# A mixture-of-experts layer on one core: the router cut by row tiles, token rows fetched through a slot table, results stored by token and choice

## The reference, cut to what matters

```
x = x + mixed @ w_out
x2 = rmsnorm(x, g_ffn)                       # 336 x 1024
logits = x2 @ w_router + b_router            # 32 experts
top_v, top_i = lax.top_k(logits, 4); gates = softmax(top_v)
# every token goes to 4 experts: 1344 (token, choice) pairs
for each expert e, over its tokens:
    gu  = xb @ w_gu[e] + b_gu[e]             # 1024 -> 2048
    hid = (clip(up, -7, 7) + 1) * min(gate, 7) * sigmoid(1.702 * gate)
    y   = hid @ w_dn[e] + b_dn[e]            # 1024 -> 1024
x = x + sum over the 4 choices of gate * y;  output rmsnorm(x, g_final)
```

## Time and profile before

| | us |
|---|---|
| median of 3 runs (lowest, highest) | 1863.03 (1858.05, 1866.95) |
| the profiled execution, its own time | 1850.85 |
| its span | 1849.3 |
| PE busy in the span | 1625.6 (88%) |
| granted TensorE clock, mean over the span | 0.946 of full |
| bytes moved by DMA | 511.30 MB, mean 276 GB/s |

### The profile page before, as it was taken

How to read it: one execution, slowest core, us unless ns; L and a number is a source line. 1 busy time by engine, 2 the same in 40 slices (tenths; PEclk the granted TensorE clock), 3 DMA queues, 4 the chain that set the end, 5 groups by cost and what they waited for, 6 DMA issues and landing times.

```text
span 1849.3 us, 20445 instructions
## 1 busy us (share of the span) xinstructions
PE 1625.6 (88%) x7088; PEld 741.2 (40%) x7089; DVE 369.4 (20%) x899; ACT 372.1 (20%) x722; POOL 116.3 (6%) x220
## 2 busy tenths in 40 slices
PE   6999999999999967988789998787999987999980
PEld 4565665566666442322223333222333322333330
DVE  3343442232321143101001111000101110110114
ACT  2443342345330020101011111011111110111111
POOL 0100000000000002000000000000000000000003
PEclk9989999899999967989999999999999998999995
DMA  6586333121235327999999899999998999599984
GB/s 221 156 220 159 111 83 114 47 75 40 92 131 209 151 114 264 409 405 410 403 412 351 336 393 408 407 410 407 363 401 326 403 412 405 217 346 402 356 337 153
DMA packets 115685, 511.30 MB, mean 276 GB/s; under 512 B 11617, under 2 KB 15566, under 8 KB 82878
## 3 DMA queue, kind: packets, MB, share of 16 engines
q1 hardware_dynamic: 98772, 454.90, 62.8%
q0 software_dynamic: 16640, 55.81, 10.6%
q10 hardware_dynamic: 234, 0.08, 0.0%
HBM read 471.21 MB, written 39.55 MB: 276 GB/s over the span
## 4 chain that ended last, share of the span: by engine, by line
PE 67%; DMA 21%; DVE 5%; issue 3%; SPq 2%; ACT 1%; POOL 0%; DVEq 0%; POOLq 0%; ACTq 0%
PE bank L535 31%; DMA ring<-in_w_gate_up 20%; PE bank L870 17%; PE bank L893 11%; PE bank L539 3%; PE bank L861 2%; PE bank L876 1%; SPq L514 1%; ACT r_kv L955 1%; DVE r_c L1221 1%; DVE r_kv L1215 1%; DVE r_qk L1215 1%; SPq L518 1%; DVE r_qk L1221 1%; DVE ring L1215 0%
## 5 line engine op out<-in xcount | busy, mean ns | idle before, releaser
L870 PE MATMUL bank<-ring,r_kv 128*64 128x512 f32 x2184 | 511.1, 613 | 65.9 <-DMA ring<-in_w_gate_up 65.8
L893 PE MATMUL bank<-ring,r_kv 128*64 128x512 f32 x1248 | 297.9, 610 | 29.7 <-ACT r_kv L955 29.7
L870 PEld LDWEIGHTS bank<-ring,r_kv 128*64 128x64 f32 x2184 | 159.7, 140 | 391.0 <-issue 298.7
L535 PE MATMUL bank<-r_xt,ring 128*128 128x336 f32 (+2 forms) x896 | 267.0, 453 | 2.0 <-DVE r_xt L1218 1.6
L1215 DVE TENSOR_SCALAR r_kv<-bank 128x512 f32<-128x512 f32 (+1 forms) x80 | 54.6, 683 | 976.9 <-PE bank L876 963.7
L535 PEld LDWEIGHTS bank<-r_xt,ring 128*128 128x128 f32 (+2 forms) x896 | 164.8, 187 | 90.7 <-issue 17.1
L893 PEld LDWEIGHTS bank<-ring,r_kv 128*64 128x64 f32 x1248 | 91.9, 142 | 206.9 <-issue 206.0
L955 ACT ACTIVATE r_xt<-bank 128x512 f32<-128x512 f32 x39 | 23.3, 597 | 507.6 <-PE bank L893 507.6
L535 PE MATMUL bank<-ring 128*128 128x336 f32 (+4 forms) x336 | 97.9, 434 | 4.1 <-DVE ring L1374 3.9
L1174 ACT ACTIVATE r_o<-r_kv 128x512 f32<-128x512 f32 x39 | 24.6, 632 | 332.7 <-DVE r_kv L1215 332.7
L1647 POOL DMA_DIRECT2D y_rows<-r_xt x78 | 41.8, 536 | 638.3 <-ACT r_xt L955 635.6
(11 more groups left out here) (213 smaller groups left out, 967.6 us busy)
## 6 DMA issues: line engine op xcount, KB each, us to landing
ring<-in_w_gate_up SPq DMA_DIRECT2D x256, 1024.0 KB, 19.4
ring<-in_w_down SPq DMA_DIRECT2D x128, 1024.0 KB, 19.2
ring<-in_w_in SPq DMA_DIRECT2D x12, 2048.0 KB, 9.1
r_v<-x_rows POOLq DMA_DIRECT2D x41, 256.0 KB, 6.7
y_rows<-r_xt POOLq DMA_DIRECT2D x78, 128.0 KB, 5.4
x_rows<-r_c POOLq DMA_DIRECT2D x7, 1024.0 KB, 6.9
x_rows<-r_c POOLq DMA_DIRECT2D x9, 768.0 KB, 8.8
y_rows<-r_c POOLq DMA_DIRECT2D x1, 5376.0 KB, 29.9
```

What stands on the lines that cost most here:

```text
L535: ins = pe.matmul(out, l, r, start=(n == 0), stop=(n == len(pairs) - 1), **kw)
L870: ins = pe.matmul(half(gate_bank if q < 2 else up_bank, q % 2), xg[:, k, :], w[:, 512 * q:512 * q + 512], start=False, stop=False, skip_gr ...
L893: ins = pe.matmul(half(out_bank, t), hidT[:, j, BLK * h:BLK * h + BLK], w[:, h, 512 * t:512 * t + 512], start=(j == 0 and h == 0), stop=(j ...
```

## The change

- **Order of the router.** PE takes `out` of tiles 0 and 1, then the router of tile 0, then `out` of tile 2, then the router of tiles 1 and 2. DVE and ACT follow in the same manner, tile by tile. The one-hot rows of a tile are one instruction of 128 elements and one reduction.
- **Tables.** One bank `pos` holds positions and counts, and two small matmuls (`pend`, `be`) give the expert of each block. New is a table of slots: DVE builds `inslot` (12 x 128) and `spread` (12 x 110), and PE multiplies them (`tab`, 12 matmuls); the result says for each slot of each block which row of `x2` it takes, and which row of `y_rows` its result goes to. Empty slots get an index past the end (slot 0 of a block always has a valid one).
- **Rows in.** POOL writes `x2` to DRAM unscattered (3 DMAs), and each block's rows come by one indirect load with a bounds check that skips indices past the end. In the loop POOL first copies the block's column of indices to `now`.
- **Rows out.** Each block's 128 half rows (2 KB each) go by one indirect store to `y_rows`, which is now ordered by token and choice; empty slots are skipped.
- **No zeros.** The filling of `x_rows` and `y_rows` is gone.
- **End.** SP loads the results in 6 plain DMAs (two choices of one tile each, 1 MB for a tile of 128), DVE waits for each pair of choices, and SP stores the outputs.

The diff, cut to its core:

```diff
-    j += [("out", t, s) for t in range(3) for s in range(2)]
-    j += [("x2T", t, s) for t in range(3) for s in range(2)]
-    j += [("lg", t) for t in range(3)] + [("pos", t) for t in range(3)] + [("cnt",)]
-    j += [("gT", t) for t in range(3)] + [("bd", t, s) for t in range(3) for s in range(2)]
+    for t in range(2):
+        j += [("out", t, s) for s in range(2)]
+    j += [("x2T", 0, 0), ("x2T", 0, 1), ("lg", 0), ("out", 2, 0), ("out", 2, 1)]
+    for t in (1, 2):
+        j += [("x2T", t, 0), ("x2T", t, 1), ("lg", t)]
+    j += [("pos",), ("pend",), ("be",), ("tab",), ("gT",)] + [("bd", t, s) for t in range(3) for s in range(2)]
...
+            nb = sp.value_load(nbi[0:1, 0:1].bitcast(I32), min_val=NE, max_val=MAXB)
+            sp.wait_ge(m_store, 16 * nb)
+            for t, (c0, m) in enumerate(ROWS):
+                for q in range(2):
+                    sp.dma_start(ring[0:m, t * SLOT + 2048 * q:t * SLOT + 2048 * q + 2048],
+                                 y_rows_dram[8 * c0:8 * c0 + 8 * m, :].rearrange("(t h) d -> t (h d)", h=8)[
+                                     :, 2048 * q:2048 * q + 2048]).then_inc(fin_y[2 * t + q], 16)
...
-            pe.wait_ge(chosen_set, 3)
+            out_rows(0)
+            out_rows(1)
+            pe.wait_ge(ld_late, 64)
+            router(0)
+            out_rows(2)
+            router(1)
+            router(2)
+            b = begin("pos")
             for t, (c0, m) in enumerate(ROWS):
-                b = begin("pos", t)
-                pairs = [(cst("ones")[0:ROWS[s][1], 0:m], chosen[0:ROWS[s][1], s, :]) for s in range(t)]
-                pairs += [(cst("below")[0:m, 0:m], chosen[0:m, t, :])]
-                end(group(b[0:m, 0:NE], pairs), "pos", t)
-            b = begin("cnt")
-            end(group(b[:, 0:NE], [(cst("ones")[0:n, :], chosen[0:n, t, :]) for t, (_, n) in enumerate(ROWS)]), "cnt")
+                pe.wait_ge(chosen_set, t + 1)
+                group(b[:, NE * t:NE * t + NE],
+                      [(cst("ones")[0:ROWS[s][1], :], chosen[0:ROWS[s][1], s, :]) for s in range(t)]
+                      + [(cst("below")[0:m, :], chosen[0:m, t, :])])
+            group(b[:, 3 * NE:4 * NE], [(cst("ones")[0:n, :], chosen[0:n, t, :]) for t, (_, n) in enumerate(ROWS)])
+            end(group(b[0:NE, 4 * NE:4 * NE + 1],
+                      [(chosen[0:n, t, :], cst("ones")[0:n, 0:1]) for t, (_, n) in enumerate(ROWS)]), "pos")
+            pe.wait_ge(nblkT_set, 1)
+            b = begin("pend")
+            end(group(b[0:NE, 0:1], [(cst("below")[0:NE, 0:NE], nblkT[:, :])]), "pend")
+            pe.wait_ge(cmpT_set, 1)
+            b = begin("be")
+            end(group(b[:, 0:NB1], [(cst("ones")[0:NE, :], cmpT[:, :])]), "be")
+            pe.wait_ge(tab_d, 1)
+            b = begin("tab")
+            end(group(b[:, 0:2 * NB1], [(inslot[0:m, 4 * t + k, :], spread[0:m, 4 * t + k, :])
+                                        for t, (_, m) in enumerate(ROWS) for k in range(4)]), "tab")
...
+            norm_x1(0)
+            norm_x1(1)
+            x2_turned(0)
+            norm_x1(2)
+            x2_turned(1)
+            x2_turned(2)
...
-                for k in range(4):
-                    step(ts(onehot[0:m, t, k, :], cst("expert")[0:m, :], topif[0:m, t, k:k + 1], ALU.is_equal))
-                c = chosen[0:m, t, :]
-                step(tt(c, onehot[0:m, t, 0, :], onehot[0:m, t, 1, :], ALU.add))
-                step(tt(c, c, onehot[0:m, t, 2, :], ALU.add))
-                signal(tt(c, c, onehot[0:m, t, 3, :], ALU.add), chosen_set, t + 1)
+                step(tt(onehot[0:m, t, :, :], cst("expert")[0:m, :].unsqueeze(1).broadcast_to([m, 4, NE]),
+                        topif[0:m, t, 0:4].unsqueeze(2).broadcast_to([m, 4, NE]), ALU.is_equal))
+                signal(dve.tensor_reduce(chosen[0:m, t, :], onehot[0:m, t, :, :].rearrange("p k e -> p e k"),
+                                         AX.X, ALU.add), chosen_set, t + 1)
...
+            dve.wait_ge(ld_late, 64)
+            for t in range(2):
+                out_rows(t)
+                norm_x1(t)
+            choose(0)
+            out_rows(2)
+            norm_x1(2)
+            choose(1)
+            choose(2)
+            filled(dve, "pos")
+            pos = bank(("pos",))
+            thr = cst("thr")
+            step(tt(cmp6[0:NE, 0, :], pos[0:NE, 4 * NE:4 * NE + 1].broadcast_to([NE, 6]), thr[0:NE, :], ALU.is_gt))
+            signal(dve.tensor_reduce(nblkT, cmp6[0:NE, 0, :], AX.X, ALU.add), nblkT_set, 1)
+            step(tt(cmp6, pos[:, 3 * NE:4 * NE].unsqueeze(2).broadcast_to([128, NE, 6]),
+                    thr.unsqueeze(1).broadcast_to([128, NE, 6]), ALU.is_gt))
+            step(dve.tensor_reduce(nblk, cmp6, AX.X, ALU.add))
             step(dve.tensor_tensor_scan(pend, cst("ones")[:, 0:NE], nblk, 0.0, ALU.mult, ALU.add))
             step(tt(start, pend, nblk, ALU.subtract))
+            take(stt(posm, start.unsqueeze(1).broadcast_to([128, 3, NE]), float(BLK),
+                     pos[:, 0:3 * NE].rearrange("p (t e) -> p t e", t=3), ALU.mult, ALU.add), "pos")
+            filled(dve, "pend")
+            take(tt(pendT, bank(("pend",))[0:NE, 0:1], nblkT, ALU.add), "pend")
+            signal(ts(cmpT, cst("block", NE), pendT, ALU.is_ge), cmpT_set, 1)
+            step(tt(prod, onehot, posm.unsqueeze(2).broadcast_to([128, 3, 4, NE]), ALU.mult))
+            step(dve.tensor_reduce(dest, prod, AX.X, ALU.add))
...
+            step(tt(valc, cst("tok"), slotc, ALU.subtract))
+            step(tt(spread[:, :, 0:NB1], inblk, valc.unsqueeze(2).broadcast_to([128, 12, NB1]), ALU.mult))
+            step(tt(val4, cst("tok4"), slotc, ALU.subtract))
+            step(tt(spread[:, :, NB1:2 * NB1], inblk, val4.unsqueeze(2).broadcast_to([128, 12, NB1]), ALU.mult))
+            signal(tt(inslot, cst("slot").unsqueeze(1).broadcast_to([128, 12, 128]),
+                      slotc.unsqueeze(2).broadcast_to([128, 12, 128]), ALU.is_equal), tab_d, 1)
...
+            filled(dve, "tab")
+            tab = bank(("tab",))
+            step(ts(idxf[:, 0, :], tab[:, 0:NB1], cst("pad")[:, 0:1], ALU.add, cst("pad")[:, 2:3], ALU.min))
+            signal(dve.tensor_copy(idx[:, 0, :].bitcast(U32), idxf[:, 0, :]), idx_set, 1)
+            take(ts(idxf[:, 1, :], tab[:, NB1:2 * NB1], 2.0, ALU.mult, cst("pad")[:, 1:2], ALU.add), "tab")
+            signal(dve.tensor_copy(idx[:, 1, :].bitcast(U32), idxf[:, 1, :]), idx_set, 2)
...
-            pool.wait_ge(rows_zeroed, 16 * 17)
-            for t, (_, m) in enumerate(ROWS):
-                pool.wait_ge(desti_set, t + 1)
-                for k in range(4):
-                    pool.indirect_dma_start(
-                        x_rows_dram[:, :], bass.IndirectOffsetOnAxis(ap=desti[0:m, t, k:k + 1].bitcast(U32), axis=0),
-                        x2[0:m, t, :], None).then_inc(x_sent, 16)
-            pool.wait_ge(x_sent, 16 * 12)
-            pool.dma_start(xrow, x_rows_dram[0:BLK, :]).then_inc(m_xrow, 16)
+            for t, (c0, m) in enumerate(ROWS):
+                pool.wait_ge(x2_ready, t + 1)
+                pool.dma_start(x_rows_dram[c0:c0 + m, :], x2[0:m, t, :]).then_inc(x_sent, 16)
+            def rows_in(column):
+                pool.indirect_dma_start(xrow, None, x_rows_dram[:, :],
+                                        bass.IndirectOffsetOnAxis(ap=column[0:BLK, :].bitcast(U32), axis=0),
+                                        bounds_check=NT - 1, oob_is_err=False).then_inc(m_xrow, 16)
+            pool.wait_ge(x_sent, 48)
+            pool.wait_ge(idx_set, 2)
+            rows_in(idx[:, 0, 0:1])
             pool.wait_ge(moe_tab, 1)
             nb = pool.value_load(nbi[0:1, 0:1].bitcast(I32), min_val=NE, max_val=MAXB)
             pool.sem_inc(yrow_free, 1)
             pool.wait_ge(m_gath, 1)
-            pool.dma_start(xrow, x_rows_dram[BLK:2 * BLK, :]).then_inc(m_xrow, 16)
+            rows_in(idx[:, 0, 1:2])
             with pool.Fori(0, nb) as b:
-                src = x_rows_dram[bass.ds(pool.snap(b * BLK + 2 * BLK), BLK), :]
-                dst = y_rows_dram[bass.ds(pool.snap(b * BLK), BLK), :]
                 pool.wait_ge(m_gath, b + 2)
-                pool.wait_ge(moe_tab, 1)
-                pool.dma_start(xrow, src).then_inc(m_xrow, 16)
+                pool.wait_ge(m_xrow, 16 * b + 32)
+                pool.sem_inc(pool_goes, 1)
+                pool.tensor_copy(now[:, 0:1].bitcast(U32), idx[:, 0, bass.ds(pool.snap(b + 2), 1)].bitcast(U32)
+                                 ).then_inc(idx_now, 1)
+                pool.wait_ge(idx_now, 2 * b + 1)
+                pool.sem_inc(pool_goes, 1)
+                rows_in(now[:, 0:1])
                 pool.wait_ge(m_yrow, b + 1)
-                pool.wait_ge(moe_tab, 1)
-                for h in range(2):
-                    pool.dma_start(dst[:, 512 * h:512 * h + 512], yrow[BLK * h:BLK * h + BLK, :]).then_inc(m_store, 16)
-                pool.wait_ge(m_store, 32 * b + 32)
```

(20 more changed lines are left out.)

180 lines of the change are left out of this document (90 added, 90 removed).

## The result

| | before | after |
|---|---|---|
| median (lowest to highest), us | 1860.54 (1858.03 to 1866.95), 4 runs | 1831.01 (1828.35 to 1831.61), 4 runs |
| the profiled execution, its own time | 1850.85 | 1828.35 |
| its span | 1849.3 | 1826.5 |

The ratio is 0.9843, interval 0.9821 to 0.9865; the medians differ by 29.5 us. The forecast was 1849 us, a gain of 14, and a range of 1834 to 1860.

The account below looks back on a forecast made before the run. The prediction had PE bound 67% of the chain and DMA 21%, mostly in the expert loop. Router 1.5, loop bytes 6.5 and end 6 sum to a gain of 14, from 1863 to 1849 us; range 1834 to 1860.

Parts of the forecast that it names:

- The early part: Before `out`: the removed zero fills were hidden behind ACT and PE, so dropping them gains 0.
- The router up to the choices: From `out` to the last choices: new tile order and cheaper one-hots, with an assumed clock drop, gain 0.5 us.
- From the choices to the loop: Counts, slot tables, gates and `bd` before the loop: it starts at 712.4 instead of 713.9, gain 1 us here.
- The loop's bytes: Expert loop: skipped empty slots (46%) save DMA time in the DMA-bound stretches, gain 6.5 us.
- I take the middle: Loop bytes: 6.5 us chosen between 0, if neighbouring slots share an engine, and the full saving.
- The upper end: Loop bytes: saving if skipped rows thin all 16 engines, 12.8 us by bytes or 15.6 by DMA engine time.
- In the others only PE counts: Expert loop: fewer bytes save time only in DMA-bound stretches (641 us); elsewhere PE alone sets the time.
- The loop's hand-overs: Expert loop: index copies and indirect DMAs come about 1 us later, but PE waits for neither; cost 0.
- The end: Behind the loop: SP's plain loads start VectorE 5.4 us earlier and its last store saves 0.5; gain 6 us.
- Both pay: Rival: skipped bytes give 13 to 15.6, router clock 3 to 8, plus the end; gain 20 to 30; chance 0.27.
- Only the end pays: Rival: skipped slots and router order save nothing, gain 6 us, total 1857; chance 0.21.
- the late store: Rival: a block's indirect store lands late, PE waits before `down` in PE-bound blocks; 18 us slower, 1881; chance 0.07.

Follow-up runs that it names:

- e7: The changed kernel with the zero fills of before written again, to DRAM nothing reads, and their waits: 1828.87 us, ratio 0.9825.
- e8: The changed kernel with the router in the order of before (all three tiles stage by stage): 1825.95 us, ratio 0.9815.
- e2: The changed kernel with full loads: empty slots load row 335 of x2, stores still skip: 1850.25 us, ratio 0.9951.
- e3: The changed kernel with full stores: empty slots are written to spare rows behind y_rows, loads still skip: 1837.84 us, ratio 0.9885.
- e9: The changed kernel with full loads landing on partitions 0-31 and 96-127, turned by a selection product; stores skip: 1850.52 us, ratio 0.9936.
- e13: The changed kernel with full loads as 128 half rows on all 128 partitions, 4 transposes of 128 x 128; stores skip: 1825.54 us, ratio 0.9821.
- e17: The kernel before, its direct loads landing as 128 half rows on 128 partitions, turned by 4 transposes; nothing skipped: 1842.21 us, ratio 0.9904.
- e1: The changed kernel with no empty slot skipped, in loads or stores: 1853.55 us, ratio 0.9969.
- e14: The changed kernel with loads as half rows on 128 partitions; loads and stores both skip: 1818.63 us, ratio 0.9793.
- e11: The changed kernel with a third router order (tile 2's `out` split around tile 1's turning; ACT copies before normalizing tile 2): 1819.47 us, ratio 0.9770.
- e6: The kernel before, unaltered, profiled a second time: 1859.22 us, ratio 0.9985.
- e18: The changed kernel with the end's DMAs (6 loads, 4 stores) issued by POOL instead of SP: 1841.61 us, ratio 0.9891.

## Why the prediction was wrong

- **The early part: 0.** Right. e7 shows it.
- **The router up to the choices: 0.5.** From the start of `out` to the end of the counts it was 67.3 us before and is 66.5, so 0.7: right in size, but by luck. With the order of before (e8) this part takes 65.0, so the cheaper choices and counts gave 2.3 and the new order, whose gain was to come from here, took 1.5 back. The clock fell in the idle stretch and came back in `out` of tile 2, as assumed (15.5 us for 16.3). The stretch between the two `out` took 7.5 instead of 5.6, as the logits of tile 0 already ran at half clock.
- **From the choices to the loop: 1.** Nothing: 28.8 us in both. `tab` started 9.8 us behind the counts (forecast 9.2) and took 5.3 to 5.5 (4.6 to 5). In e8 the same tables took 26.2 us, since PE was at full clock for a few microseconds there; "`tab` wakes the clock" was named as a bound and happens with e8's order only.
- **The loop's bytes: 6.5.** This is the step that failed: 20.8. Three things were wrong in it.
  - "I take the middle" rested on an end of 0, should neighbouring slots share an engine; e2 and e3 show that both skips pay.
  - The upper end, 12.8 by bytes or 15.6 by the queue's time, priced a loaded row at its own packet. It costs more, since the weights beside it slow from 314 to 513 ns while rows land on partitions 0 to 63. e2 shows the size (19 us for the loads, against 7 for the stores), e9, e13 and e17 the cause.
  - "In the others only PE counts" left out the 25 us blocks with full DMA engines. 11.6 of the 20.8 us came out in the blocks that enter the bound runs. The bound blocks themselves went to 31.45 us in the mean, which is the 31.4 that I gave for "all bytes count". The 641 us were also no count of bound blocks: 17 blocks of before took over 28 us, not 20, and add up to 534 us; the first stretch, from 748 us, begins with 34 us in which PE sets the pace.

  The indirect form with its copies costs 2 to 5 us (e1's loop, 1093.1, against 1088.0 and 1090.9), which I had at 0.
- **The sentences on the Trainium skill's "The descriptor swizzle"** (DMA: Bandwidth & Descriptors) had the store thin the engines evenly, worth 6.4, and the load not at all. The store's skip measured 7; the load's, once the landing costs nothing beside itself, 4 (e13 against e14), and 19 as it stood.
- **The loop's hand-overs: 0.** Right: PE-bound blocks stayed at 25.0 and no wait for a store appeared.
- **The end: 6.** 8.0. VectorE starts 5.9 earlier (5.4 forecast). The last store gave 2.1 instead of 0.5: only POOL's work of issuing had been counted, and not POOL's DRAIN of 1.54 us behind the landing, nor the landing itself (2.9 us with POOL, 2.6 with SP).
- **The rivals.** "Both pay" had the sum (20 to 30, measured 29.5) but not its parts, so that was luck: the bytes gave more than its 15.6 and the router next to nothing for its 3 to 8. "Only the end pays" and the late store are excluded by e1 and the timeline.

What is shown: a landing on partitions 0 to 63 slows the transfers of the weights beside it, the reading place and the direct or indirect form do not take that away, and landing on as many partitions in 0-31 and 96-127 or on all 128 ends it. What is only argued: that the reason is the number of ways into the memory, as the Trainium skill, SBUF — State Buffer, section "Door 1: The DMA port swizzle (why `[64,N]` ≈ `[32,N]`)", has it; the runs tell where, not why.

## What to carry to other kernels

When the DMA engines are full, don't price a transfer by its queue's share alone: look at the rate (GB/s) in the few microseconds in which it lands, since a small transfer to partitions 0 to 63 can slow the large ones beside it. Spread it over all 128 partitions before trying to make it smaller. Don't count the bytes of the bound stretches alone either: where the engines are full in the stretch ahead, bytes saved there count too. When work is reordered to fill an idle stretch, check the helper engines' order too: against the plain order of e8 the changed kernel's order lost 4 us, and e11's gained 6. e11 altered the lists of PE, ACT and VectorE at once, so what each gave isn't shown.

## What the runs showed of the hardware

- A landing of 256 KB on partitions 0 to 63 takes the rate of the 16 engines together down to 288 to 293 GB/s in the mean (e2, e6); on partitions 0-31 and 96-127 it stays at 414 (e9), on all 128 at 406 to 408 (e13, e14, e17). The DMA share reads 1.00 to 1.05 in the windows of both kinds, so it does not show this.
- The six blocks moved 417 to 418 GB/s once loads landed well (e9, e13, e14, e17), where 404 to 412 had looked like the ceiling.
- An index past the end leaves a packet of a few bytes (9 ns for the 8-byte ones in e2): 1367 packets under 512 B in 142 us of the changed kernel (other small ones among them), with 2.1% of the engines' time for the whole queue.
- POOL's DRAIN at the end of the program took 1.54 us in the kernel before and 8.16 in the changed one (8.97 in e18), SP's 0.01 us (after).
- The same program can start a stretch 5 us earlier or later (617.9 and 623.3). Most of it is the clock: ahead of `out` it stood at half for 37.5 us in the first profile of before and for 44 in the second, an estimated 3.4 of the 5.5 us. One profile's span is no measure for a change of this size; the stretches between are (96.0 and 96.0).
